# Experts on compact slots: tokens sorted by expert, 31 experts ranked by load into 20 units

## The reference, cut to what matters

```python
hf = h.reshape(-1, d_)                                   # 256 x 1024
pg = softmax(hf @ w_rg + b_rg)                           # 4 groups
pg_top, g_idx = lax.top_k(pg, 1)
e_sel = take_along_axis(e_logits, g_idx[:, :, None], axis=1)[:, 0]
pe_top, j_idx = lax.top_k(softmax(e_sel), TOP_K)         # 2 of the group's 8
weights = pg_top * pe_top / sum(pe_top)
e_idx = g_idx * EXPERTS_PER_GROUP + j_idx
combine = sum(one_hot(e_idx, 32) * weights[..., None], axis=1)
for e in range(32):                                      # 1024 -> 2 x 256 -> 1024
    act = silu(hf @ w_gate[e]) * (hf @ w_up[e])
    y = y + combine[:, e:e + 1] * (act @ w_down[e])
```

## Time and profile before

| | |
|---|---|
| median of 3 runs | 1917.04 us (1915.57 to 1919.29) |
| span of the profiled execution | 1915.7 us; the record gives no other time of that execution |
| expert stage | from 1554.3 us, when the last logits are in PSUM, to the end: 361.4 us, 19% |
| loads of the expert stage | 96 chunks of 1 MiB, 100.7 MB |

### The profile page before, as it was taken

One profiled execution on the slowest core, in us unless ns is written; L12 is line 12 of the kernel. 1 busy time (PEld: TensorE's weight loads), 2 busy tenths in 40 slices (PEclk: granted clock), 3 DMA queues, 4 the chain that ended last, 5 costly groups with the idle time before them and its releaser, 6 DMA issues. The chain is left out here.

```text
span 1915.7 us, 33026 instructions
## 1 busy us (share of the span) xinstructions
PE 1863.9 (97%) x13514; PEld 1612.6 (84%) x13514; DVE 1280.1 (67%) x1879; ACT 994.8 (52%) x1555; POOL 111.5 (6%) x133
## 2 busy tenths in 40 slices
PE   8999997999999999999979999999999999999999
PEld 6888896999888888889869998888989987777787
DVE  6675787675666666667867765665888855344896
ACT  5444682554544454447635544443766544334784
POOL 1000006000000000000050000000021000000000
PEclk9999998999999999999989999998999999999999
DMA  9764430343666566654305545653444236776994
GB/s 389 297 231 186 155 133 25 150 160 132 252 230 231 183 228 246 222 187 154 111 4 185 190 155 210 262 208 130 154 145 142 89 153 236 285 298 275 359 367 159
DMA packets 53185, 378.68 MB, mean 198 GB/s; under 512 B 5992, under 2 KB 6176, under 8 KB 7856
## 3 DMA queue, kind: packets, MB, share of 16 engines
q1 hardware_dynamic: 44592, 320.30, 45.1%
q0 software_dynamic: 8448, 56.32, 7.5%
HBM read 375.53 MB, written 1.06 MB: 197 GB/s over the span
## 5 line engine op out<-in xcount | busy, mean ns | idle before, releaser
L354 DVE TENSOR_TENSOR weights_split<-ring,weights_split 128x1024 fp32r<-128x1024 f32 x456 | 539.9, 1227 | 165.1 <-ACT weights_split L344 164.9
L344 ACT CAST weights_split<-ring 128x1024 fp32r<-128x1024 f32 x456 | 454.4, 1049 | 179.9 <-PE ps L377 164.9
L375 PE MATMUL ps<-weights_split,act 128*128 128x512 f32 (+1 forms) x896 | 333.3, 372 | 1.4 <-DVE weights_split L354 1.2
L377 PE MATMUL ps<-weights_split,act 128*128 128x512 f32 (+1 forms) x896 | 328.5, 367 | 0.0
L376 PE MATMUL ps<-weights_split,act 128*128 128x512 f32 (+1 forms) x896 | 328.0, 366 | 0.0
L2339 DVE TENSOR_TENSOR expert_split<-ring,expert_split 128x1024 fp32r<-128x1024 f32 x144 | 169.7, 1221 | 48.7 <-ACT expert_split L2263 46.3
L375 PEld LDWEIGHTS ps<-weights_split,act 128*128 128x128 f32 x896 | 168.4, 188 | 29.7 <-issue 2.3
L377 PEld LDWEIGHTS ps<-weights_split,act 128*128 128x128 f32 x896 | 168.3, 188 | 28.3
L376 PEld LDWEIGHTS ps<-weights_split,act 128*128 128x128 f32 x896 | 168.6, 188 | 26.2
L375 PE MATMUL ps<-act,weights_split 128*128 128x256 f32 x608 | 174.0, 286 | 0.3
L376 PE MATMUL ps<-act,weights_split 128*128 128x256 f32 x608 | 169.8, 279 | 0.0
(11 more groups left out here) (553 smaller groups left out, 3494.1 us busy)
## 6 DMA issues: line engine op xcount, KB each, us to landing
ring<-stream SPq DMA_DIRECT2D x300, 1024.0 KB, 4.8
stretch<-ada_in POOLq DMA_DIRECT2D x24, 1024.0 KB, 5.2
small_weights<-stream POOLq DMA_DIRECT2D x12, 1024.0 KB, 7.8
tokens_room<-stream POOLq DMA_DIRECT2D x12, 1024.0 KB, 7.8
y<-c_in POOLq DMA_DIRECT2D x4, 512.0 KB, 6.3
act_room<-mem_in SPq DMA_DIRECT2D x2, 1024.0 KB, 4.8
consts<-w_consts SPq DMA_DIRECT2D x1, 1280.0 KB, 11.6
x<-x_in SPq DMA_DIRECT2D x1, 1024.0 KB, 5.3
```

Source lines behind the costliest of these rows:

```text
L344: core.nc.scalar.copy(self.hi[:, self.place(i), part], core.slot(chunk)[:, part]).then_inc(self.rounded.sem, 1)
L354: core.nc.vector.tensor_tensor(self.lo[:, self.place(i), part], core.slot(chunk)[:, part], self.hi[:, self.place(i), part].bitcast(F32), A ...
L375: nc.tensor.matmul(out, lhs[0], rhs[0], start=start, stop=False, **kw)
L377: return nc.tensor.matmul(out, lhs[1], rhs[0], start=False, stop=stop, **kw)
```

## The change

Each token's two assignments now get slots of their own. The 512 assignments are sorted by expert, and each expert has only the slots that its tokens need.

- **Expert 0** is computed for all 256 tokens, as two "F" units in token order. Its three chunks no longer depend on the routing. They come with the stream of `second_stage`, which also splits two of them.
- **The other 31 experts** are ranked by their number of tokens. Rank r can have at most 512 / (r + 1) tokens. Ranks 0 to 2 get two units of 128 slots, 3 to 6 one each ("L": 10 units, split way). Ranks 7 to 14 share units in pairs, 64 slots each ("P": 4 units), and ranks 15 to 30 in fours, 32 slots each ("Q": 4 units). P and Q are made in the plain way, with two or four matmuls of 64 or 32 output rows side by side, straight from the loaded weights.
- **Loads** are by rank, with a register for each rank's first chunk. L chunks come whole. For P the chunks of two experts come in two halves each (512 KiB, 4 KB a partition), for Q those of four experts in quarters (256 KiB, 2 KB a partition), so that a place of 1 MiB holds the same quarter of four experts. There are 7 places: the ring, a sixth one, and half of the room of the tokens. POOL loads nothing any more.
- **Slots**: `gather_slots` writes all 512 slots to `compact` in SBUF, and each unit copies a window of it, whose start is read from a register: ACT and DVE for L, POOL for P and Q.
- **Way back**: after every unit its sums are rounded and subtracted (`round_sums`, `subtract_sums`), and `scatter` adds them to the tokens in PSUM with 16 matmuls; DVE makes the matrix for that (`way_back`) and the share of each slot (`shares_of`) per unit.

The diff, cut to its core:

```diff
+UNIT_ORDER = "F F L0 Q L0 L1 Q L1 L2 Q L2 L3 P L4 P L5 P L6 P Q"
+SLOTS_IN_ALL = RING + 2
+def split_places():
+    behind, at, room = [[] for _ in range(2 * UNITS + 4)], 2 * UNITS + 3, 3
+    for i in reversed(range(len(SPLIT_LOADS))):
...
+            at = min(at, (2 * u - 3, 2 * u - 2, 2 * u + 3)[phase])
+            while len(behind[at]) >= room:
+                at -= 1
...
 @block.sync
             sp.wait_ge(ordered.sem, ordered.at(1))
-            for j in range(EXPERT_CHUNKS):
...
+            for n, (u, phase, i) in enumerate(LOADS):
+                of, ranks, _ = EXPERT_UNITS[u]
+                if ranks[0] not in first:
+                    for rank in ranks:
+                        first[rank] = sp.value_load(first_chunk[0:1, rank:rank + 1], ...)
+                freed = SLOT_PLACES[n][1]
...
+                width = CCOLS // len(ranks)
+                for at, rank in enumerate(ranks):
+                    source = core.stream[first[rank] + (MOE_AT + phase), :, i * width:(i + 1) * width]
+                    sp.dma_start(slot(n)[:, at * width:(at + 1) * width], source).then_inc(landed.sem, 16)
 @block.tensor, gate_up of a P or Q unit
+                for i in range(n):
+                    load = LOAD_AT[u, part, i]
+                    await_slot(pe, load)
+                    w = slot(load).rearrange("p (e k n) -> p e k n", e=n, n=2 * STEP)
+                    for k in range(4 // n):
+                        ch = 4 * part + i * (4 // n) + k
+                        for e in range(n):
+                            ins = nc.tensor.matmul(ps[e * width:(e + 1) * width, u % 2, :],
+                                                   a_whole[:, window_slot(u), ch, e * width:(e + 1) * width], w[:, e, k, :],
+                                                   start=ch == 0, stop=ch == KB - 1, skip_group_check=True)
+                    ins.then_inc(whole_done.sem, 1)
 @block.tensor, order
-            keep_busy(core, 2, 8)
-            pe.wait_ge(chosen.sem, chosen.at(1))
             for k in range(KB):
                 gather_near(k)
+            pe.wait_ge(chosen.sem, chosen.at(1))
+            for t in range(TT):
+                nc.tensor.matmul(count_row, ones, taken[:, t, :], ...)
...
             gate_up(0, 0)
+            pe.wait_ge(placed.sem, placed.at(1))
+            nc.tensor.matmul(chunk_row, ones[0:32, :], rows[0:32, 2, :], ...).then_inc(chunks_placed.sem, 1)
...
             gate_up(0, 1)
...
+            for u in range(UNITS + 1):
                 if u + 1 < UNITS:
                     gate_up(u + 1, 0)
+                if u < UNITS:
+                    turn_hidden(u)
                 if u == 0:
+                    for k in range(KB):
+                        gather_slots(k)
+                elif u == 1:
+                    spread_keys()
+                else:
+                    scatter(u - 2)
                 if u + 1 < UNITS:
                     gate_up(u + 1, 1)
                 if u >= 1:
                     down_proj(u - 1)
+            scatter(UNITS - 1)
 second_stage
-            core.refill(sp, start, n - RING)
+            core.refill(sp, start, n - RING + 3 * FIXED)
-                if c + ways < n:
+                if c + ways < n + 2:
                     weights.subtract(dve, c + ways)
```

More of the change, by code:

```diff
@@ L34 @@
 PER_GROUP = EXPERTS // GROUPS
[L35 to L38, removed]
 W = 512
@@ L137, in expert_chunks @@
[L137 to L163, removed]
@@ L166 @@
[L166 to L173 removed]
+FIXED = 1
@@ new lines, with expert_units @@
+ROUTED = EXPERTS - FIXED
+CHOICES = 2
+ASSIGNED = CHOICES * S
+UNIT_ORDER = "F F L0 Q L0 L1 Q L1 L2 Q L2 L3 P L4 P L5 P L6 P Q"
+SLOTS_IN_ALL = RING + 2
+ROUTE_AT = {}
+ROUTE_COLS = 0
+def expert_units(order):
+    units, pairs, quads, tokens, begun = [], 0, 0, 0, {}
+    for word in order.split():
+        kind = word[0]
+        if kind == "F":
+            units.append(("F", (), tokens))
+            tokens += 1
+        elif kind == "L":
+            rank = int(word[1:])
+            units.append(("L", (rank,), begun.get(rank, 0)))
+            begun[rank] = P
+        elif kind == "P":
+            units.append(("P", (7 + 2 * pairs, 8 + 2 * pairs), 0))
+            pairs += 1
+        else:
+            units.append(("Q", tuple(range(15 + 4 * quads, 19 + 4 * quads)), 0))
+            quads += 1
+    return units
@@ new lines, in expert_loads @@
+def expert_loads():
+    loads, known = [], set()
+    for u, phase in phase_order():
+        kind, ranks, _ = EXPERT_UNITS[u]
+        if kind == "L" and (ranks, phase) not in known:
+            known.add((ranks, phase))
+            loads.append((u, phase, 0))
+        elif kind in "PQ":
+            loads += [(u, phase, i) for i in range(len(ranks))]
+    return loads
+LOADS = expert_loads()
+SPLIT_LOADS = [load for load in LOADS if EXPERT_UNITS[load[0]][0] == "L"]
+WHOLE_LOADS = [load for load in LOADS if EXPERT_UNITS[load[0]][0] != "L"]
@@ new lines, with slot_plan @@
+BEHIND_SUMS, BEHIND_HIDDEN = split_places()
+def slot_plan():
+    free = [((MOE_AT + j) % RING, ("stream", MOE_AT + j - RING)) for j in range(3 * FIXED, RING)]
+    free += [(RING, None)]
+    free += [((MOE_AT + j) % RING, ("stream", MOE_AT + j)) for j in range(3 * FIXED)]
+    free += [(RING + 1, ("gather", 0))]
+    places, landed, filled = [], [], [0] * SLOTS_IN_ALL
+    for n, (u, phase, i) in enumerate(LOADS):
+        slot, freed = free.pop(0)
+        filled[slot] += len(EXPERT_UNITS[u][1])
+        places.append((slot, freed))
+        landed.append(filled[slot])
+        load = (u, phase, i)
+        done = ("split", SPLIT_LOADS.index(load)) if load in SPLIT_LOADS else ("whole", WHOLE_LOADS.index(load))
+        free.append((slot, done))
+    return places, landed, filled
@@ L2400, in _ @@
             split_tokens(0)
+            split_tokens(1)
+            for k in range(KB):
+                split_near(k)
             dve.wait_ge(route_loaded.sem, route_loaded.at(16))
[L2402 to L2406 removed]
```

972 lines of the change are left out of this document (539 added, 433 removed).

## The result

The changed kernel takes 1892.87 us (median of 4 runs, 1886.86 to 1893.82) against 1917.24 beside it: 24.4 us less, a ratio of 0.9874, 95% interval 0.9851 to 0.9896. The forecast was 55 us less. The time lies in the range of 1844 to 1900, and outside the forecast's own range of 1850 to 1880.

The account below looks back on a forecast made before the run. DMA was to replace PE as the stage's bound (256 against 236 us): first landing 1582.3, plus 249.5 for loads with 13 of waits, 26 serial, 3.4 and 1.3 more, gives 1862 us; range 1844 to 1900, own range 1850 to 1880.

Parts of the forecast that it names:

- rival D: Q matmuls: 32 output rows overlap badly, 0.2275 us an instruction instead of 0.12, time near 1885 us; chance 0.05.
- The seam: In `second_stage`: four more half splits, 2 x 2.4 us on DVE, are covered by 8.8 us of idle DVE, cost 0.
- Rival C: Q loads: quarter rows collide, halving the rate, 2.75 us more a chunk, 132 us, time near 1980; chance 0.07.
- the price of a load: Expert stage's loads: 2.75 us for every chunk, 93 in 256 us, with 0 extra for the small form.
- rival B: Q loads: small loads stream slower, 3.6 us a chunk instead of 2.75, 41 us more, time 1880 to 1900; chance 0.16.
- The sign that the prediction had named for B or C: In the Q units: a DMA share of 1 at less than 330 GB/s would show slower small loads or colliding rows.
- The overlap of the waits: Before L units: split waits of 4.8, 3 to 4 and 1 to 1.5 us overlap with DMA's time.
- PE's sum: PE's work in the expert stage: 236 us after the change, where it had 361.
- Rival A: Expert stage: PE sets the end, 236 us plus 25 of waits, loads hidden, time 1837 to 1845; chance 0.12.
- DMA's stands: Loads waiting for places: 3 us at loads 7 and 8, 5.5 at load 9, 4 to 5 later, 13 taken.
- The head: Stage start: the experts' order is known at 1574 to 1576.5, first load at 1577.5, 17 us later than before.
- The end: Behind the last L unit's down chunk: 26 us of serial splits, products, sums and ways back, then 3.4 us.

Follow-up runs that it names:

- one_dma: Changed kernel with each P or Q load as one whole 1 MiB chunk of one expert, wrong weights: 1878.7 us, ratio 0.9799.
- pairs: Changed kernel with each Q load holding half of the columns of two experts, rows of 4 KB: 1889.9 us, ratio 0.9877.
- one_dma_2k: Changed kernel with each P or Q load as one 1 MiB transfer in short rows, the first expert's piece repeated for all: 1911.3 us, ratio 0.9974.
- few_bytes: Changed kernel with P and Q loads bringing only the first expert's piece, read by all experts' matmuls, 45 MiB instead of 93: 1856.6 us, ratio 0.9695.
- six_places: Changed kernel with six places for chunks instead of seven, the extra one gone: 1900.3 us, ratio 0.9915.
- splits: Changed kernel with split work moved forward on ACT and DVE, before unit 2 and in the later units: 1876.2 us, ratio 0.9794.
- few_splits: Changed kernel with P and Q loads of the first expert's piece alone and all split work moved forward: 1839.6 us, ratio 0.96.
- split_first: Changed kernel with only unit 2's first chunk rounded before the slots are copied and subtracted before the window: 1886.1 us, ratio 0.9849.
- head_early: Changed kernel with the matmul that turns ranks into chunk numbers ahead of the first half of unit 0: 1892.3 us, ratio 0.9874.
- rows_8k: Changed kernel with as many transfers, each of 32 or 64 whole 8 KB rows into as many partitions, wrong weights: 1971.4 us, ratio 1.031.
- tail: Changed kernel with the last three units' down products reordered, so only unit 19's down product, sums and way back follow the last load: 1888.0 us, ratio 0.9862.
- single: Changed kernel with one expert's whole chunk to a Q load, P loads changed the same way: 1930.7 us, ratio 1.0083.

## Why the prediction was half right

**Right.** The direction: PE's work fell, the DMA share rose to 0.94, PE stands in the P and Q units for loads, and the Q matmuls keep the pace of the earlier trace rows, 0.115, so rival D's condition doesn't hold. The seam costs nothing visible. Rival C is out: quarter rows cost 3.0 us a chunk, not 5.5.

**The steps that failed** are two: the price of a load, which is the largest part of the 27.8 us missing in the sum (11), and the claim that waits for splits cost next to nothing.

**The price of a load** was mis-sized. I took 0 for the small form and 2.75 for every chunk; as busy time of DMA the runs have 2.66, 2.82 and 3.0 us for rows of 8, 4 and 2 KB, which makes 21 x 2.66 + 24 x 2.82 + 48 x 3.0 = 267.5 instead of 256. So rival B's direction was right, at 0.25 us a Q chunk above 2.75 instead of its 0.85. `one_dma` shows that the form is worth 14 us of time. The stores of the earlier trace rows, from which I took that the form has no price, were four separate transfers and could not show a rate. The 2.75 itself came from windows with a share of 0.96 and 0.97; busy time for whole chunks is less, 2.66. The Trainium skill ("DMA: Bandwidth & Descriptors", Rules for kernel authors) warned against transfers below 1 MiB, and in direction the runs agree: 3.0 against 2.66 us a MiB. The sign that the prediction had named for B or C, a share of 1 at less than 330 GB/s in the Q units, is there in places (0.98 at 302 from 1655 to 1660 us). The 500 us that the prediction worked out from the page's fit for a single DMA are far off for a queue: all 93 MiB took 267. Whether the size of a transfer or the length of its rows decides is open: `pairs` changes both, and `one_dma_2k` has a price of its own.

**The overlap of the waits** is the sentence on ACT and DVE: "Where DMA is the bound these overlap with its time, since the places are refilled later but not idle for long." The waits themselves were counted well (4.8 us before unit 2, measured 5.05; 3 to 4 behind Q units, measured 2.2 to 2.7; 1 to 1.5 behind P units, measured 0.9 to 1.0). That they cost little was wrong: taking 11 us of them away gave 15 to 17. The two paths through the stage stand too close for one of them to hide the other. Without the bytes PE's path takes 300 us (`few_bytes`, 1847.0 - 1546.66), and 287 with the splits moved. The path of the loads has 26.6 of head, 267 at full share and 20 from the last landing to the end, 314. And seven places of 2.87 us let one run only 20 us ahead of the other. In the units of four DMA holds PE; in the large units PE and the splits hold the places. Each stop of either passes to the other, so the stage takes longer than the longer of the two: 334. `six_places`, `splits` and the longer stands of DMA in `one_dma` all show this coupling.

**PE's sum** was too low as well, without effect on the forecast. Rival A took 236 us of PE and 25 of waits; in `few_bytes`, which answers to it, PE was busy for 251.1 at a granted clock of 0.96 and waited 18.0 + 5.8 + 0.9 = 24.7 for splits, sums and the selection. That `few_splits` lands in A's range is luck: its waits are 10 us shorter, which makes up for most of what the sum of PE lacked.

**DMA's stands**: 13 us taken, about 20 measured, 8 with `splits`. An early one is large (share 0.39 from 1605 to 1615 us), because the eighth load waits for the split of unit 2's first chunk; with `split_first` DMA stood 6 us less.

**The head** came 4.0 us late (the first half of unit 0 ran at half the pace, 0.43 us a product; the granted clock was 0.62 up to the first load), but with `head_early` the first load went out 5 us earlier and the time stayed, so no run shows that this term counts.

**The end**: 34.6 instead of 29.4. The clock was 0.75 there, and the ways back took 2.93 and 2.90 us where I had 1.9. I had put 0 to 8 for this into the range and 0 into the sum.

What stays open: what makes the few long packets of the short rows, the number of transfers, four chunks being read side by side or the length of the queue; `rows_8k` was meant to tell and met another limit. Also why `tail` gave at most 5 us and not 10 to 14.

## What to carry to other kernels

When a change brings PE and DMA to nearly the same sum, with a few buffers between them, add their waits instead of taking the larger sum, count head and end with the path that they belong to, and price each step that frees a buffer, here a 2.2 us delay on DVE, as time on the path. To see what one side needs, run it once with the other side's work cut to a fraction: the gap between that time and the real one tells what can be won by overlap alone. A faster head gave nothing here, since the first buffer that must be reused came free no earlier; a better transfer form did, even though part of its gain went into longer stands. And compare runs made at different times by their ratios to one kernel measured beside each, not by medians: two gains of 3 and 5 us here were noise.

## What the runs showed of the hardware

- Loads in rows of 8, 4 and 2 KB a partition (transfers of 1 MiB, 512 and 256 KB) took 2.66, 2.82 and 3.0 us of DMA busy time a MiB over the stage. The median packet gives 2.47, 2.54 and 2.69; a stretch of 2 KB rows alone moved 394 GB/s, another 302.
- Transfers of 256 KB into 32 partitions, four to a place, kept the DMA share at 1.02 and moved only 224 GB/s, against 425 for whole chunks (`one_dma`, 1655 to 1680 us, share 1.01). The Trainium skill ("DMA: Bandwidth & Descriptors", The descriptor swizzle) describes, for one transfer to 128 partitions, that partitions 0 to 63 are written by one half of the engines through one half of the ports. Half of the engines doesn't fit here, since all 16 were busy; half of the ports would fit the rate, but no run here shows the ports.
- An issue by SP took 0.33 us, but up to 4.3 with a full queue (the row below, from the changed kernel: min, median, max in ns). During the longest DMA moved 427 GB/s at a share of 1.01, so nothing was lost there; what the others cost no run tells.

```profile
L2169 SPq DMA_DIRECT2D ring<-stream x187: 332/333/4319, 1577.6 to 1856.6; - x187
```

- Matmul records with 32 output rows and 512 columns (float32): four that go to different rows start almost together, the next four 0.43 us later, 0.115 each; records on the same rows start 0.43 apart, and with eight in a row on the same rows the next rows' overlap them, 0.22 each on average (`single`).
